# Weight slots moved to other SBUF addresses in a two-layer decoder kernel

## The reference, cut to what matters

```python
for i in range(DEPTH):                       # DEPTH = 2
    h = rmsnorm(x, norm1[i])
    mix, xq = mlstm_mixer(...) if i % 2 == 0 else diff_attention(...)     # both start with h @ w_in
    xo = memory_cross_attention(xq, mem, ...)                             # mem @ w_mem_kv inside
    x = x + concat([mix, xo]) @ w_out[i]                                  # 1024 x 1024
    h = rmsnorm(x, norm2[i])
    gu = h @ w_gate_up[i]                                                 # 1024 x 5632
    x = x + (silu(gu[..., :2816]) * gu[..., 2816:]) @ w_down[i]           # 2816 x 1024
```

## Time and profile before

| | us |
|---|---|
| median of 3 runs | 1203.16 |
| lowest and highest | 1203.13, 1204.05 |
| the profiled execution, device time | 1204.02 |
| the profiled execution, span of its instructions | 1202.2 |

### The profile page before, as it was taken

One profiled execution on the slowest core, in us unless ns is written; L12 is line 12 of the kernel. 1 busy time (PEld: TensorE's weight loads), 2 busy tenths in 40 slices (PEclk: granted clock), 3 DMA queues, 4 the chain that ended last, 5 costly groups with the idle time before them and its releaser, 6 DMA issues.

```text
span 1202.2 us, 18736 instructions
## 1 busy us (share of the span) xinstructions
PE 1196.8 (100%) x6998; PEld 1032.9 (86%) x6998; DVE 755.9 (63%) x1099; ACT 502.4 (42%) x1012; POOL 857.4 (71%) x873
## 2 busy tenths in 40 slices
PE   9999999999999999999999999999999999999998
PEld 7888887788889998899888777778888899889997
DVE  7954434645737991599335888874674599348931
ACT  7522456733203551355231666644431255125510
POOL 7998433566878996699676444445688799669965
PEclk9999999999999999999999999999999999999999
DMA  7234211132223333233433222232232333322332
GB/s 282 92 123 157 71 36 53 53 106 79 92 83 106 106 106 123 88 106 106 126 103 97 80 71 71 64 80 69 71 100 79 118 106 107 105 89 98 115 105 85
DMA packets 35097, 117.43 MB, mean 98 GB/s; under 512 B 4417, under 2 KB 4930, under 8 KB 34886
## 3 DMA queue, kind: packets, MB, share of 16 engines
q1 hardware_dynamic: 33416, 112.83, 29.2%
q10 hardware_dynamic: 1598, 3.51, 1.2%
HBM read 111.07 MB, written 2.11 MB: 94 GB/s over the span
## 4 chain that ended last, share of the span: by engine, by line
PE 97%; DVE 1%; ACT 1%; issue 0%; ACTq 0%; POOL 0%; POOLq 0%
PE PS L1946 69%; PE PS L2284 26%; PE PS L2385 1%; DVE Al L1564 0%; PE PS L2194 0%; PE PS L2413 0%; PE PS L2354 0%; DVE nmB L1850 0%; PE PS L2019 0%; PE PS L2346 0%; PE PS L2338 0%; DVE PB L1862 0%; ACT tmp L1010 0%; ACT tmp L1018 0%; DVE PB L1861 0%
## 5 line engine op out<-in xcount | busy, mean ns | idle before, releaser
L783 POOL TENSOR_TENSOR w_lo<-w_raw,w_hi 128x256 fp32r<-128x256 f32 (+1 forms) x516 | 394.7, 796 | 11.0
L778 POOL TENSOR_SCALAR w_hi<-w_raw 128x1024 fp32r<-128x1024 f32 (+2 forms) x132 | 142.1, 1076 | 283.4 <-PE PS L1946 275.0
L2284 PE MATMUL PS<-tc_hi,w_hi 128*128 128x256 f32 x896 | 250.9, 280 | 0.0
L2284 PE MATMUL PS<-tc_hi,w_lo 128*128 128x256 f32 x896 | 250.0, 279 | 0.0
L2284 PE MATMUL PS<-tc_lo,w_hi 128*128 128x256 f32 x896 | 250.0, 279 | 0.0
L1946 PE MATMUL PS<-Hh,w_hi 128*128 128x512 f32 x560 | 229.3, 410 | 0.0
L1946 PE MATMUL PS<-Hl,w_hi 128*128 128x512 f32 x560 | 219.1, 391 | 0.0
L1946 PE MATMUL PS<-Hh,w_lo 128*128 128x512 f32 x560 | 219.0, 391 | 0.0
L1946 PE MATMUL PS<-Ah,w_hi 128*128 128x512 f32 (+1 forms) x544 | 208.0, 382 | 0.1
L1946 PE MATMUL PS<-Ah,w_lo 128*128 128x512 f32 (+1 forms) x544 | 205.0, 377 | 0.0
L1946 PE MATMUL PS<-Al,w_hi 128*128 128x512 f32 (+1 forms) x544 | 204.9, 377 | 0.0
(11 more groups left out here) (300 smaller groups left out, 1805.5 us busy)
## 6 DMA issues: line engine op xcount, KB each, us to landing
w_raw<-in_wt_dram SPq DMA_DIRECT2D x181, 512.0 KB, 3.6
w_raw<-in_wt_dram SPq DMA_DIRECT2D x16, 384.0 KB, 3.0
w_raw<-in_wt_dram SPq DMA_DIRECT2D x8, 448.0 KB, 3.3
QKR<-QKP ACTq DMA_DIRECT2D x24, 128.0 KB, 4.8
xT<-in_x_t_dram SPq DMA_DIRECT2D x8, 256.0 KB, 4.8
out_dram<-xT SPq DMA_DIRECT2D x8, 256.0 KB, 2.0
mT<-in_mem_t_dram SPq DMA_DIRECT2D x1, 1024.0 KB, 9.5
cn<-in_constants_dram SPq DMA_DIRECT2D x1, 594.5 KB, 6.9
```

What stands on the lines that cost most here:

```text
L778: nc.gpsimd.tensor_scalar(w_hi[:, sl, 0:nk], w_raw[:, raw, 0:nk], 0.0, 1.0, ALU.add, ALU.mult).then_inc(w_round, 1)
L783: lo = nc.gpsimd.tensor_tensor(w_lo[:, sl, w], w_raw[:, raw, w], w_hi[:, sl, w].bitcast(F32), ALU.subtract)
L2284: last = nc.tensor.matmul(out_, w[:, b + k], a[:, q, k], start=q < 4 and k == 0 and j == 0, stop=k == 3 and j == 2, skip_group_check=q > 3)
```

## The change

It puts unused bytes between SBUF tiles and between the slots, and addresses the slots and blocks accordingly. No instruction is added, removed, reordered or resized on any engine: with line numbers left out, the built programs read the same on all five, and every access to `w_hi` and `w_lo` has the same length and stays contiguous. Only start addresses differ. From the two built programs, bytes in a partition:

| tile | before | after | before, modulo 512 | after, modulo 512 |
|---|---|---|---|---|
| `Hh` | 17536 | 17536 | 128 | 128 |
| `Hl` | 33920 | 33920 | 128 | 128 |
| `Ah` | 50304 | 50432 | 128 | 256 |
| `Al` | 66688 | 66816 | 128 | 256 |
| `w_raw` | 83072 | 83200 | 128 | 256 |
| `w_hi` slots 0, 1, 2, last 4 blocks | 99456 + 4096 s | 99776 + 4160 s | 128 in all | 448, 0, 64, 128 |
| `w_lo` slots 0, 1, 2, last 4 blocks | 113792 + 4096 s | 114624 + 4160 s | 128 in all | 448, 0, 64, 128 |
| `cn` | 128128 | 129152 | 128 | 128 |
| `tc_hi`, `tc_lo` | 169152, 197824 | 170176, 198848 | 192 | 192 |
| `PB` | 181440 | 182464 | 192 | 192 |
| `VB`, `ATB` | 177344, 191680 | 178368, 192704 | 192 | 192 |
| `wg` | 218112 | 219136 | 0 | 0 |

All tiles behind `w_lo` move by 1024 bytes. Chunks (2048 or 1024 bytes) and blocks (512 bytes) are multiples of 512, so the last two columns hold for every chunk and block of a tile.

```diff
--- before.py
+++ after.py
@@ -120,6 +120,7 @@
 HI_ENTRY = [4, 6, 0, 1, 5, 2, 3]
 TOKENS = 13
 SHARED = 2
+W_STEP = 8 * P + 16
 
 
 def bq_tile(c):
@@ -276,13 +277,27 @@
         xT = sb("xT", [P, KD, SEQ])
         Hh = sb("Hh", [P, KD, SEQ], F32R)
         Hl = sb("Hl", [P, KD, SEQ], F32R)
+        sb("shift_a", [P, 32])
         Ah = sb("Ah", [P, 8, SEQ], F32R)
         Al = sb("Al", [P, 8, SEQ], F32R)
         w_raw = sb("w_raw", [P, RAW, 8, P])
-        wq_hi = sb("w_hi", [P, 28, P], F32R)
-        wq_lo = sb("w_lo", [P, 28, P], F32R)
-        w_hi = wq_hi[:, 0:8 * SPLIT].rearrange("p (s k) m -> p s k m", k=8)
-        w_lo = wq_lo[:, 0:8 * SPLIT].rearrange("p (s k) m -> p s k m", k=8)
+        sb("shift_hi", [P, 48])
+        wf_hi = sb("w_hi", [P, SPLIT * W_STEP + 4 * P], F32R)
+        sb("shift_lo", [P, 80])
+        wf_lo = sb("w_lo", [P, SPLIT * W_STEP + 4 * P], F32R)
+
+        def tile_slots(ap):
+
+            full = ap[:, 0:SPLIT * W_STEP].rearrange("p (s x) -> p s x", x=W_STEP)
+            return full[:, :, 0:8 * P].rearrange("p s (k m) -> p s k m", m=P)
+
+        def quarter_blocks(ap):
+
+            first = [(b // 8) * W_STEP + (b % 8) * P for b in range(0, 28, 4)]
+            return [ap[:, f:f + 4 * P].rearrange("p (k m) -> p k m", m=P) for f in first]
+
+        w_hi, w_lo = tile_slots(wf_hi), tile_slots(wf_lo)
+        wq_hi, wq_lo = quarter_blocks(wf_hi), quarter_blocks(wf_lo)
         cn = sb("cn", [P, N_CON])
         ones = sb("ones", [P, P])
         gcol = sb("gcol", [P, N_PRM])
@@ -745,7 +760,7 @@
             def weight_low(n, p, q):
                 b = block_of(pair_at(n)[0], q)
                 pool.wait_ge(s_round, weight_round(p, q))
-                nc.gpsimd.tensor_tensor(wq_lo[:, b:b + 4], pair_source(n, q), wq_hi[:, b:b + 4].bitcast(F32),
+                nc.gpsimd.tensor_tensor(wq_lo[b // 4], pair_source(n, q), wq_hi[b // 4].bitcast(F32),
                                         ALU.subtract).then_inc(s_low_p, 1)
 
             for n in range(2, N_TILES):
@@ -1096,7 +1111,7 @@
                         act.wait_ge(product, 6 * (p - 1) + q + 1)
                     else:
                         act.wait_ge(dense_done, n - 1 + q // 2 if q < 4 else n - KD + 1)
-                    nc.scalar.activation(wq_hi[:, b:b + 4], pair_source(n, q), ACT.Copy).then_inc(s_round, 1)
+                    nc.scalar.activation(wq_hi[b // 4], pair_source(n, q), ACT.Copy).then_inc(s_round, 1)
 
                 def shared_hi(n):
 
@@ -1701,7 +1716,7 @@
 
                     n, p, b = seg_base(l, s) + 2 * i, pair_number(l, s, i), block_of(l, q)
                     dve.wait_ge(s_round, weight_round(p, q))
-                    nc.vector.tensor_tensor(wq_lo[:, b:b + 4], pair_source(n, q), wq_hi[:, b:b + 4].bitcast(F32),
+                    nc.vector.tensor_tensor(wq_lo[b // 4], pair_source(n, q), wq_hi[b // 4].bitcast(F32),
                                             ALU.subtract).then_inc(s_low_v, 1)
 
                 def pair(s, i):
@@ -2281,7 +2296,7 @@
                     b = block_of(l, q)
                     for k in range(4):
                         for j, (w, a) in enumerate(((wq_hi, tc_hi), (wq_hi, tc_lo), (wq_lo, tc_hi))):
-                            last = nc.tensor.matmul(out_, w[:, b + k], a[:, q, k], start=q < 4 and k == 0 and j == 0,
+                            last = nc.tensor.matmul(out_, w[b // 4][:, k], a[:, q, k], start=q < 4 and k == 0 and j == 0,
                                                     stop=k == 3 and j == 2, skip_group_check=q > 3)
                     last.then_inc(dense_done if q == 6 else product, 2 if q == 6 else 1)
```

## The result

The change makes the kernel slower: 1211.88 us (median of 4 runs, 1211.31 to 1213.49) against 1203.61 us (4 runs, 1203.13 to 1204.20), a ratio of 1.0071 with a 95% interval from 1.0053 to 1.0088. The forecast was 1195.8 us. The profiled execution took 1213.49 us.

A forecast was written before the change was run, and what follows sets the result against it. PE was taken as the bound: number of matmuls times distance between starts. Gains of 6.9 and 0.4 us, pairs 0, gave 1204.02 - 7.3 = 1196.7 us profiled, 1195.8 by the median; range 1165 to 1212 us.

The forecast's parts named there:

- What bounds the kernel: Whole kernel: PE is busy throughout, so time is the number of matmuls times the distance between two starts.
- The 512-column tiles: H and A tiles, 3120 matmuls: leaving D = 0 saves 2.2 ns each, 6.9 us gained.
- The bound for the loss: 512-column tiles: at most 8.3 ns lost per matmul at D 384, read from the gate tile's 235 ns.
- The modulus: All matmuls: D, address of the next weights less that of the moving operand, was taken modulo 512.
- The 256-column A tiles: 192 matmuls on Ah and Al: 2.2 ns gained each, 0.4 us.
- The pairs: FFN pair stages, 2688 matmuls: taken as 0, between 15.8 us gained and 5.9 us lost.
- POOL and DVE: Work on moved tiles unchanged, effect 0; POOL's 796 ns low part would have to grow by 40 ns to be seen.
- Rival 1: No effect of D at 512 columns or in the pairs: 1203.2 us, at most 0.4 less; chance 0.22.
- Rival 2: Distances from 192 to 384 remove most of the surplus: 58.9 us gained, 1144.3 us, half of it 1173.7; chance 0.22.
- Rival 3: D = 384 is bad, 8.3 ns on 1491 H and pair matmuls: 12.4 us lost, 1215.6 or 1208.3 us; chance 0.24.

The follow-up runs named there:

- e4: Kernel before with both weight tiles 256 bytes further on, so D is 256 for H and A, 192 for pairs: 1203.46 us, ratio 1.0003.
- e2: Changed kernel with slots back at 4096 bytes, starts still moved; D 320 for H, 192 for A, 256 for pairs: 1221.39 us, ratio 1.0149 to the kernel before.
- e10: Kernel before with the last 4 blocks of w_hi and w_lo (seventh quarter of each pair) moved to D = 0: 1198.64 us, ratio 0.9967.
- e1: Changed kernel with slots of 4160 bytes alone, tile starts as before modulo 512: 1209.69 us, ratio 1.0056 to the kernel before.
- e11: Kernel before with the seventh quarter of each pair at D = 128, its blocks 192 bytes further on: 1203.53 us, ratio 1.0007.
- e3: Kernel before with only tc_hi and tc_lo 128 bytes further on, pairs at D = 320: 1202.48 us, ratio 0.9998.
- e8: Kernel before with second and third matmul of each plain-tile triple loading 64 weight columns instead of 128: 1207.26 us, ratio 1.0036.

## Why the prediction was wrong

- **What bounds the kernel: right.** PE has no break in the stages, its count is the same, and the change acted through the distance alone.
- **The 512-column tiles: this step failed.** The prediction said "I take the 2.2 ns that leaving D = 0 shows for the same type at 256 columns: 3120 x 2.2 = 6.9 us gained". Leaving 0 costs 2 to 6 ns there; the same term measured is 9.2 us lost. At 256 columns 0 is the slowest place and at 512 the fastest. The bound for the loss, 8.3 ns from the gate tile, was on the table and held 233.3 - 226.7 = 6.6 ns; the forecast took the bound's other side by the row of another shape, though the only row with 512 columns off D = 0 spoke for a loss. That row was also read too broadly: during the second of its two matmuls a block of `w_hi` is loaded, which is D = 0, so only one of each two distances of 235 ns is one at 384.
- **The modulus: wrong, a half.** I argued for 512 from the steps of blocks and chunks, which excludes 1024 and 2048 but not 256. By 256 the 656 A matmuls at D = 256 never left the good place (227.4 ns), as e4 shows for all tiles.
- **The 256-column A tiles: right in sum, 0.4 us, and not by the place alone.** Their means, waits of up to 260 ns included, went from 121.8 to 118.6 ns at 192, from 120.8 to 120.6 at 256 and from 119.6 to 115.9 at 320. The 2.2 ns for each was an average of unequal ones.
- **The pairs: 0 was forecast, 0.5 us lost came, but by cancelling:** 1.4 us lost at 256, 1.5 gained at 320, 0.6 lost at 384. The prediction treated 256 as a new place; it is the 120.0 ns place. The gain at 320 is the fast rhythm in part of these quarters.
- **POOL and DVE: right.** 801 against 796 ns is far from the 40 ns named, and DVE's busy time fell by 4.2 us.
- **Rival 1, no effect:** fell at both widths. The sentence in the Trainium skill, page "SBUF — State Buffer", section "SBUF: two separate sides", by which PE waits for nobody, isn't contradicted by another engine's traffic here; but e2 and e4 show that the time depends on how far PE's own two reads lie apart, by 18.5 us with one set of distances and by nothing with another. The rival's own support was overstated: before the change whole H tiles have 226.7 to 227.9 ns, not the same to 0.2.
- **Rival 2, large gain:** fell. No distance tried at 512 columns is better than 0. The part with the pairs has something in it, 113.3 ns, but it comes with how the stream enters a place and not with the place, and DVE stops it at about 1 us a stage.
- **Rival 3, slower:** its sign held and its place only in part. D = 384 costs 4.2 ns on 723 H matmuls, not 8.3, and 0.8 on the pairs, so by its own account (it decided from 4.9 ns) it would not have turned the sum. The sum turned because the other tiles, forecast to gain, lost too, D = 320 most.

## What to carry to other kernels

Where a stream of matmuls with a load each has no break, compare the distance of starts by (weights' address - moving address) modulo 256 before pads go in: whole multiples of 256 are the place for 512 columns, and one pad between equal slots is enough to lose it. Of the distances tried here no other kept 226.7 ns. Take the price of a place only from rows of the same column count, and look at it tile by tile, since a mean can hide two rhythms, at 512 columns (229 and 233.3) as at 256. What a faster stream then meets is the shortest chain of waits inside the unit, here DVE's joins, and not the engine with the most busy time.

## What was unexpected of the hardware

- At 512 columns of fp32r the distance is 226.7 ns in a stream at D = 0 or 256, 233.1 to 234.2 at 32, 64, 96, 160, 224 and 320, and 232.1 to 232.4 at 128 and 384. At 192 and 448 it is 229 or 233.3: e2 has both at the same D. At 256 columns it is 120.0 at 0 and 256, about 118.5 at 32, 128 and 384, and 116.7 at 224.
- At 256 columns and a D of 64, 192, 320 or 448 there are two rhythms, 117.8 and 113.3 ns, and each goes on until something disturbs it. Behind D = 0 it was 113.3 in 27 of 28 pairs of e10 and in e1, but 117.8 behind 256 in layer 0 of the change. Behind D = 128 it was 117.8 (e1, e11). Straight from 512 columns it was 117.8 in e1, e3, e11, e10's first pairs and layer 1 of the change, but 113.3 in two of e8's four stages. A wait of 0.1 us or more ended the fast one in 17 of 20 pairs of e10, and not behind three waits in e8's first stage. What picks the rhythm stays open, and so does the one slow pair of e10 behind D = 0.
- The 13.3 ns that 512 columns take above 213.3 went with no distance tried, nor with shorter loads. Their origin stays open.
